# Row products with the weights outer and the token halves inner, and one 1024-column add per tile on VectorE

## The reference, cut to what matters

```python
# feed-forward part of the first block, D_FF = 2816 = 22 tiles of 128
u = h @ w_ffn_up[l]
a, b = u[..., :D_FF], u[..., D_FF:]
a = causal_dwconv(a, ffn_conv_w[l], ffn_conv_b[l])
x = x + (jax.nn.silu(a) * b) @ w_ffn_down[l]

# merge at the end of each of the two layers, D_MODEL = 1024 = 8 tiles of 128
merged = (jax.nn.sigmoid(ga) * (ya @ w_br_a) + jax.nn.sigmoid(gb) * (yb @ w_br_b)
          + jax.nn.sigmoid(gc) * (yc @ w_br_c))
x = x + merged @ w_out[layer]
return rmsnorm_2(x, final_norm_g)     # after the last layer; each layer and block starts with a norm of x
```

## Time and profile before

| what | value |
|---|---|
| median of three runs | 3788.7 us |
| the profiled execution | 3791.21 us, span 3789.4 us |
| mean granted TensorE clock, share of full speed | 0.969 |
| PE busy | 3533.9 us, 93% |
| DVE busy | 1814.6 us, 48% |
| ACT, POOL busy | 799.1 us, 1183.5 us |
| row adds L2103 | 608 of 690 ns |
| matmuls of the row products L857 | 1824 |

### The profile page before, as it was taken

One profiled execution on the slowest core, in us unless ns is written; L12 is line 12 of the kernel. 1 busy time (PEld: TensorE's weight loads), 2 busy tenths in 40 slices (PEclk: granted clock), 3 DMA queues, 4 the chain that ended last, 5 costly groups with the idle time before them and its releaser, 6 DMA issues.

```text
span 3789.4 us, 56884 instructions
## 1 busy us (share of the span) xinstructions
PE 3533.9 (93%) x22988; PEld 2821.5 (74%) x22988; DVE 1814.6 (48%) x2496; ACT 799.1 (21%) x1250; POOL 1183.5 (31%) x563
## 2 busy tenths in 40 slices
PE   5999699999999999699999999999799999999996
PEld 4788499788888888467777678887577667688885
DVE  5431566546766667643443533443524444424434
ACT  3311433221010010233222320000322222300001
POOL 2233054234344344221122224344212121134431
PEclk9999799999999999799999999999899999999998
DMA  2111000211111111210000021111200000121111
GB/s 89 34 66 44 1 4 4 82 61 45 50 50 44 50 50 44 72 52 22 23 22 28 28 77 46 50 50 45 96 23 23 28 28 23 33 78 50 44 50 56
DMA packets 38876, 167.13 MB, mean 44 GB/s; under 512 B 4304, under 2 KB 4816, under 8 KB 37456
## 3 DMA queue, kind: packets, MB, share of 16 engines
q1 hardware_dynamic: 36432, 135.85, 11.6%
q10 hardware_dynamic: 2304, 29.23, 1.9%
HBM read 150.39 MB, written 14.68 MB: 44 GB/s over the span
## 4 chain that ended last, share of the span: by engine, by line
PE 87%; DVE 9%; issue 2%; ACT 1%; DMA 0%; DVEq 0%; POOL 0%; ACTq 0%; SPq 0%; POOLq 0%
PE ps L395 53%; PE ps L857 11%; PE ps L1164 5%; PE ps L983 3%; PE ps L687 3%; PE ps L1014 2%; PE ps L1032 2%; DVE sc L2245 2%; DVE sq_sum L1668 1%; PE ps L1053 1%; PE ps L944 1%; DVE hL L1681 1%; DVE xT L2103 1%; PE ps L415 1%; PE ps L407 1%
## 5 line engine op out<-in xcount | busy, mean ns | idle before, releaser
L308 POOL TENSOR_TENSOR wH<-wraw,pv 128x1024 fp32r<-128x1024 f32 x242 | 461.0, 1905 | 2339.2 <-PE ps L395 1914.7
L395 PE MATMUL ps<-hH,wH 128*128 128x512 f32 x2832 | 899.0, 399 | 30.2 <-DVE hL L1681 21.1
L395 PE MATMUL ps<-hL,wH 128*128 128x512 f32 x2832 | 884.1, 394 | 0.0
L395 PE MATMUL ps<-hH,wL 128*128 128x512 f32 x2832 | 883.3, 393 | 0.0
L395 PEld LDWEIGHTS ps<-hH,wH 128*128 128x128 f32 x2832 | 531.6, 190 | 161.8 <-issue 26.5
L310 POOL TENSOR_TENSOR wL<-wraw,wH 128x1024 fp32r<-128x1024 f32 x242 | 619.3, 2559 | 19.0
L395 PEld LDWEIGHTS ps<-hL,wH 128*128 128x128 f32 x2832 | 534.8, 190 | 114.4 <-issue 1.5
L395 PEld LDWEIGHTS ps<-hH,wL 128*128 128x128 f32 x2832 | 533.8, 189 | 112.7 <-issue 0.8
L2103 DVE TENSOR_TENSOR xT<-ps,xT 128x512 f32<-128x512 f32 x608 | 411.0, 690 | 50.2 <-PE ps L857 47.7
L2331 DVE TENSOR_TENSOR sg<-ps,sg 128x1024 f32<-128x1024 f32 x48 | 58.8, 1224 | 494.1 <-PE ps L1164 494.1
L1543 ACT ACTIVATE sc<-sc,stat 128x256 f32<-128x256 f32 (+7 forms) x256 | 171.0, 668 | 149.4 <-DVE stat L2252 78.9
(11 more groups left out here) (338 smaller groups left out, 4201.9 us busy)
## 6 DMA issues: line engine op xcount, KB each, us to landing
wraw<-ws SPq DMA_DIRECT2D x242, 512.0 KB, 3.5
park<-xT ACTq DMA_DIRECT2D x2, 4096.0 KB, 12.4
xT<-park ACTq DMA_DIRECT2D x2, 4096.0 KB, 12.2
xT<-xin SPq DMA_DIRECT2D x1, 4096.0 KB, 12.2
xT<-xin ACTq DMA_DIRECT2D x1, 4096.0 KB, 12.7
out<-xT SPq DMA_DIRECT2D x8, 512.0 KB, 3.0
park<-yH ACTq DMA_DIRECT2D x1, 2048.0 KB, 7.9
yH<-park ACTq DMA_DIRECT2D x1, 2048.0 KB, 10.3
```

The source lines that it names most:

```text
L308: pool.tensor_tensor(wH[:, j, :], wraw[:, j, :], zero, ALU.add).then_inc(w_hi, 1)
L395: mm = pe.matmul(pair(p)[:, half * HALF:(half + 1) * HALF], wp, hp[:, k, half * HALF:(half + 1) * HALF], start=(m == 0 and n == 0), stop=( ...
```

## The change

The two token halves become the inner loop in `row_gemm`, as in `col_gemm`; the signal after the first half is gone. `row_add` waits once per row for all six matmuls and does one add of 1024 columns over both banks. Line numbers behind L2095 fall by up to 8, so the add L2103 is L2096 in the changed kernel.

```diff
@@ row_gemm
                     pe.wait_ge(sem("row_added"), n + e + 7)
-                    for half in range(2):
-                        for m, (w, h) in enumerate(((wH, hi), (wH, lo), (wL, hi))):
+                    for m, (w, h) in enumerate(((wH, hi), (wH, lo), (wL, hi))):
+                        for half in range(2):
                             mm = pe.matmul(pair(2 + e % 2)[:, half * HALF:(half + 1) * HALF],
                                            w[:, j, e * P:(e + 1) * P], h[:, half * HALF:(half + 1) * HALF],
                                            start=(m == 0), stop=(m == 2))
-                        if half == 0:
-                            mm.then_inc(sem("row_half"), 1)
                     mm.then_inc(sem("row_done") if e < KT - 1 else gemm_done[j], 1)
@@ row_add
                 for e in range(KT):
-                    for half in range(2):
-                        if half == 0:
-                            dve.wait_ge(sem("row_half"), n + e + 1)
-
-                            dve.wait_ge(sem("row_added"), n + e + 1)
-                        elif e < KT - 1:
-                            dve.wait_ge(sem("row_done"), rows * (KT - 1) + (e + 1))
-                        else:
-                            dve.wait_ge(gemm_done[j], use + 1)
-                        x = xT[:, e, half * HALF:(half + 1) * HALF]
-                        ins = dve.tensor_tensor(x, bank(4 + 2 * (e % 2) + half), x, ALU.add)
-                    ins.then_inc(sem("row_added"), 1)
+                    dve.wait_ge(sem("row_added"), n + e + 1)
+                    if e < KT - 1:
+                        dve.wait_ge(sem("row_done"), rows * (KT - 1) + (e + 1))
+                    else:
+                        dve.wait_ge(gemm_done[j], use + 1)
+                    dve.tensor_tensor(xT[:, e, :], pair(2 + e % 2), xT[:, e, :], ALU.add).then_inc(sem("row_added"), 1)
```

## The result

The changed kernel takes 3817.84 us (median of six runs, 3816.82 to 3818.61) where the kernel before takes 3789.13 us (median of six runs, 3786.07 to 3791.13). The ratio is 1.0075, 95% interval 1.0064 to 1.0085: slower by 28.7 us. The forecast was +21.8 us, that is 3810.5 us, in a range of 3800 to 3821.

The account below looks back on a forecast made before the run. PE was taken to bound the kernel (93% busy, 87% of the chain of waits). Pairs +13.1, merge products +7.4, last pair +0.9 and layer ends +0.4 gave +21.8 us, 3810.5 us; own range 3806 to 3815, wider 3800 to 3821.

Parts of the forecast that it names:

- VectorE's saving is hidden: Row adds on VectorE: busy time falls by 48 us, but gains nothing where PE sets the pace.
- The matmul order costs nothing by itself: Row matmuls on PE: still six a row, in the order of `col_gemm` at 0.2267 us each, costed at nothing.
- The wait it lengthens: From a row's end through the add back to PE: 1.04 us becomes 1.575, pausing PE at every second row.
- Merge products: Fourteen merge products inside the loops: three pauses in 8 rows, +0.525 us each, +7.4 us in all.
- Feed-forward pairs: Ten feed-forward pairs: seven pauses in 16 rows, less 0.19 us lost already, +1.31 us each, +13.1 us.
- What lies behind a pause costs nothing: Work after an added pause (VectorE, POOL, weight DMAs, ACT): moves with PE or has spare time, costed at nothing.
- The three products with norms: Last feed-forward pair, +0.9 us, and the last product of each layer, +0.2 us each, +0.4 us.
- The clock: PE's granted clock in the changed stretches: stays at 1.00, 2.4 GHz, despite the pauses; nothing added.
- Rival 1: Row adds: PE waited for VectorE's fixed cost, so no pauses arise; about -6 us, 3783 us; chance 0.06.
- Rival 2: Merge products: the new order brings 0.2267 us a matmul instead of 0.2333; +19 us, 3808 us; chance 0.12.
- Rival 3: Handover from PE to VectorE: 0.30 us, making each pause 0.11 longer; +34 us, 3823 us; chance 0.08.
- Rival 4: Pauses of PE: real, but hidden slack or jitter takes up half; about +11 us, 3800 us; chance 0.08.

Follow-up runs that it names:

- the table of add lengths: The changed kernel with each add cut from 1024 columns to 896, 768 or 640, the rest not added: 3803.3, 3793.4 and 3786.2 us against 3817.8.

## Why the prediction was right

- *VectorE's saving is hidden*: right. 46 us of busy time went and nothing came of it.
- *The matmul order costs nothing by itself*: right for the changed kernel (23.65 us with either order). Alone, with two adds kept, it does cost, 0.54 us a pair, but that isn't the change as made.
- *The wait it lengthens*: right. Handovers 0.20 and 0.17 us where 0.19 and 0.16 were taken, the add 1.225 as taken, one held row in two. "None at 3, 5, 7" came out so in the pair shown, but from row 9 on the odd rows are held somewhat too, since a tie between an odd row's add and the end of the row before was taken as free. The 239 waits against 115 counted don't mean 239 pauses: most are weight loads that start late.
- *Merge products*: forecast +0.525 us each, measured +0.55. Held rows are 2.98 us apart, as 1.575 + 1.40 gives:

```profile
2301.70 0.73 PE L857 MATMUL ps<-mH,wH 128*128 128x512 f32 x2
2304.68 0.73 PE L857 MATMUL ps<-mH,wH 128*128 128x512 f32 x2
```

- *Feed-forward pairs*: the term that was mis-sized, +1.31 forecast, +1.67 measured, 3.6 us over ten. Held rows are 2.98 us apart here too, where 1.575 + 1.36 gives 2.935, and the two rows after the last hold take 0.09 us more than 2.72. Of the 0.36 us, 7 x 0.02 = 0.14 is the longer handovers. The rest is R: I took the pace of undisturbed matmuls, 0.2267 us, for the rows behind a hold, and there they run at up to 0.233, nearly as in the merge. The trace of before had only a hint of it, the longer 0.50 us matmul at a hold in a pair 0.19 us longer, of which the hold itself is 0.16.
- *What lies behind a pause costs nothing*: right. `col_gemm` beside the pairs and merge products takes 43.52 and 10.88 us as before.
- *The three products with norms*: +0.9 and +0.4 forecast. The profiles have +1.1 and +0.3. The first has the right sign, but kernels with the same code there differ by up to 2.3 us; the second is within the spread and not shown.
- *The clock*: right for pairs and merge products, 1.00 throughout.
- Of the 28.7 us, 24.4 are in the pairs and merge products, 1.4 in the products with norms, which is uncertain, and the other 2.9 can't be placed, since single executions differ by more than that elsewhere. The time is 2.8 us above the forecast's own range of 3806 to 3815 and inside the wider one.

Rival 1 (VectorE's fixed cost is what PE waits for) is excluded by the table of add lengths, and with it the gain that the Trainium skill's rule on fixed latency per instruction ("VectorE: DVE Perf Modes", the section on the TRN2 errata) would promise if VectorE's busy time set the end. Rival 2 is excluded: the merge pace didn't change with the order (11.75 us both ways); it hung on an address. Rival 3 had the right direction with too long a handover, 0.30 us against 0.20. Rival 4 (half of the pauses taken up by slack) is excluded by pairs and merge products that grew by more than was forecast.

## What to carry to other kernels

When two engines hand buffers back and forth, compare one number with another: from the end of one piece of work through the consumer's whole instruction and both handovers, against the producer's time for the pieces that the other buffers allow. Merging two consumer instructions into one moves the whole instruction behind the producer's end and can pass that line while the consumer's busy time falls; either leave room, or add a buffer. Here 0.03 us of room wasn't enough and 0.17 us nearly was, since the producer prepares its next piece ahead of time (a weight load, 0.22 us ahead). And when one stage runs the same instructions at another pace than its neighbour, look at the operands' addresses.

## What the runs showed of the hardware

- A 128x512 fp32r matmul of the merge products follows the one before after 0.2333 us when its moving operand (mH, mL) starts at an odd multiple of 64 bytes, and after 0.2267 us when it starts at a multiple of 128 bytes: 11.20 and 10.88 us for 48, moved by 64 bytes and nothing else.
- A wait that is met with only 0.03 us of room delays the weight load of a feed-forward row (0.18 us ahead of its matmul instead of 0.22), and the matmuls run at about 0.2325 instead of 0.2267 us; with 0.17 us of room they keep their pace (pairs 22.11 and 21.79 us). In the merge, whose matmuls run at 0.2333 us anyway, weight loads that start 0.19 us ahead instead of 0.23 cost nothing.
- A held matmul runs as if started 0.16 to 0.17 us after the end of the add that it waits for, and an add starts 0.19 to 0.20 us after the next row's first matmul.
